# Layer 2 of an encoder trunk on 8 cores: another order of folding, statistics, gate tiles and shift transfers

## The reference, cut to what matters

```python
for i in range(DEPTH):
    shift, scale, gate = ada_modulation(c, w_ada[i], b_ada[i])   # silu(c) @ w + b, three parts
    h = rms_norm(x, g_norm[i]) * (1.0 + scale) + shift
    ...
    elif kind == 2:                      # layer 2, the one changed
        a, ag, z = jnp.split(jnp.einsum('bsd,de->bse', h, w_in_c), 3, axis=-1)
        glu = a * jax.nn.sigmoid(ag)
        ext, conv_c_new = with_history(glu, hist_c, CCONV_W - 1)       # 31 taps, depthwise
        y = causal_depthwise_conv(ext, w_conv_c) + b_conv_c
        y = jax.nn.silu(layer_norm(y, ln_c_g, ln_c_b))                 # over 2048 channels
        out = jnp.einsum('bse,ed->bsd', y * jax.nn.silu(z), w_out_c)
    x = x + gate * out
```

## Time and profile before

| what | value |
|---|---|
| median of 3 runs | 2197.24 us (2192.96 to 2240.93) |
| profiled execution | 2198.0 us, span 2196.5 us on core 0 |
| other cores' spans | 2178.1 to 2191.1 us |
| busy, core 0 | PE 94%, PE weight load 59%, DVE 48%, ACT 31%, POOL 14% |
| layer 2, g = 0 | about 1172 to 1498 us |
| layer 2, g = 1 | about 1498 to 1820 us |

### The profile page before, as it was taken

How to read it: one execution, slowest core, us unless ns; L and a number is a source line. 1 busy time by engine, 2 the same in 40 slices (tenths; PEclk the granted TensorE clock), 3 DMA queues, 4 the chain that set the end, 5 groups by cost and what they waited for, 6 DMA issues and landing times.

```text
span 2196.5 us, 38718 instructions; the slowest of 8 cores (2178.1 to 2196.5 us)
## 1 busy us (share of the span) xinstructions
PE 2073.5 (94%) x15725; PEld 1295.2 (59%) x15725; DVE 1044.8 (48%) x1463; ACT 685.4 (31%) x891; POOL 316.9 (14%) x605
## 2 busy tenths in 40 slices
PE   3999999999999999999999998999998999999996
PEld 1645666456666666666666664556564556666663
DVE  3454240542555554555545232555332657747745
ACT  3264313543011121111121434532445532222341
POOL 1001101011001000001003441103441100000000
PEclk9999999999999999999999999999999999999998
DMA  9836848078346543346446986667886743433347
GB/s 208 155 102 103 138 72 136 14 132 138 57 74 104 89 77 68 60 73 110 77 80 122 201 180 142 114 108 150 173 185 128 137 103 68 77 69 68 78 68 208
DMA packets 94064, 244.02 MB, mean 111 GB/s; under 512 B 17088, under 2 KB 42048, under 8 KB 93632
## 3 DMA queue, kind: packets, MB, share of 16 engines
q0 software_dynamic: 54992, 188.11, 48.6%
q1 hardware_dynamic: 38896, 53.43, 9.2%
HBM read 344.92 MB, written 13.76 MB: 163 GB/s over the span
## 4 chain that ended last, share of the span: by engine, by line
PE 83%; DMA 8%; DVE 3%; SPq 2%; ACT 2%; issue 2%; POOL 0%; DVEq 0%; ACTq 0%; POOLq 0%
PE ps L505 74%; PE ps L750 4%; DMA ring<-w_ada 2%; SPq L162 2%; PE ps L1120 2%; DMA ysT<-tmp 2%; DMA w_fold<-ring 1%; DMA ring<-w_in_a 1%; PE ps L1004 1%; PE ps L395 1%; DMA ring<-w_in_c 1%; PE ps L451 0%; DMA xa_sb<-xa 0%; PE ps L877 0%; DMA tmp<-tmp 0%
## 5 line engine op out<-in xcount | busy, mean ns | idle before, releaser
L505 PE MATMUL ps<-hT,ring 128*128 128x352 bf16 (+1 forms) x8448 | 1300.4, 315 | 22.0 <-DMA ring<-w_in_a 6.0
L505 PEld LDWEIGHTS ps<-hT,ring 128*128 128x128 bf16 x8448 | 826.0, 98 | 490.1 <-issue 40.3
L505 PE MATMUL ps<-ysT,ring 128*128 128x352 bf16 (+1 forms) x3072 | 470.4, 313 | 12.8 <-DVE xb_sb L594 5.1
L505 PEld LDWEIGHTS ps<-ysT,ring 128*128 128x128 bf16 x3072 | 297.8, 97 | 185.0 <-issue 21.4
L162 POOL DMA_DIRECT2D tmp<-tmp x256 | 129.5, 555 | 116.9 <-PE ps L1148 71.1
L750 PE MATMUL ps<-ring,hT 128*128 128x512 bf16 x544 | 123.6, 385 | 3.5 <-DMA ring<-w_in_a 2.7
L1073 DVE TENSOR_TENSOR tmp<-tmp,ps 128x1074 bf16<-128x1074 f32 (+3 forms) x64 | 45.5, 711 | 167.6 <-PE ps L505 160.9
L940 ACT ACTIVATE tmp<-ps 128x1074 f32<-128x1074 f32 (+1 forms) x32 | 33.9, 1059 | 263.7 <-PE ps L505 263.7
L951 DVE TENSOR_TENSOR tmp<-tmp,ps 128x1074 f32<-128x1074 f32 (+3 forms) x64 | 45.4, 709 | 140.4 <-PE ps L505 129.4
L1128 ACT ACTIVATE tmp<-ps,cst_sb 128x16 bf16<-128x16 f32 (+2 forms) x160 | 69.8, 437 | 111.4 <-PE ps L1120 87.8
L588 DVE SCALAR_TENSOR_TENSOR xb_sb<-ps,modT,xb_sb 128x1056 f32<-128x1056 f32 x32 | 42.2, 1317 | 119.6 <-PE ps L505 119.2
(11 more groups left out here) (182 smaller groups left out, 1619.9 us busy)
## 6 DMA issues: line engine op xcount, KB each, us to landing
ring<-w_in_b POOLq DMA_DIRECT2D x64, 512.0 KB, 5.3
ring<-w_ada POOLq DMA_DIRECT2D x48, 512.0 KB, 11.9
ring<-w_in_a POOLq DMA_DIRECT2D x48, 512.0 KB, 12.7
ring<-w_in_c POOLq DMA_DIRECT2D x48, 512.0 KB, 5.8
ring<-w_in_d POOLq DMA_DIRECT2D x24, 512.0 KB, 5.3
tmp<-tmp SPq DMA_DIRECT2D x128, 69.4 KB, 5.4
tmp<-tmp POOLq DMA_DIRECT2D x128, 69.4 KB, 5.7
tmp<-tmp SPq DMA_DIRECT2D x128, 67.5 KB, 5.0
```

The lines of the kernel that those rows point to most:

```text
L505: ins = h.matmul(PSB[:, 3 * sl + n, 0:W], lhsT=lw, rhs=rh[:, n * W:(n + 1) * W], start=(first and k == 0), stop=(last and k == len(pairs) ...
```

## The change

It has five parts. (1) In the loop, `square` and `stats` run five tiles behind instead of four; tile 11 is done in the tail. (2) Of the 16 shift transfers of a tile, 6 go over SP and 10 over POOL instead of 8 and 8. (3) The tail has another order; the first fold and the first batch of the second are emptied by DVE instead of ACT; the second fold's ring slots are taken after `zmm(4)`, its later batches come one gate tile later. (4) After `root`, the silu table is loaded by a one-column activation. (5) Part 1 of layer 3's modulation moves to hook 5 of layer 1, g = 1, and part 2 to hook 3 of layer 3, g = 0.

```diff
-        def batch(k):
-            if k == 0:
-                got["w"] = [get(sp) for sp in wspec]
-                got["o"] = [get(sp) for sp in ospec]
+        def take():
+            got["w"] = [get(sp) for sp in wspec]
+            got["o"] = [get(sp) for sp in ospec]
+
+        def batch(k, eng):
...
-                s.op("act", lambda h, o=o, hf=hf: h.activation(out=v3(o, 8)[:, 2 * k:2 * k + 2, :], in_=PSB[:, 3 * sl:3 * sl + 2, 256 * hf:256 * hf + 256], func=AF.Copy),
-                     writes=sk(sl) + [ok])
+                o, src = v3(o, 8)[:, 2 * k:2 * k + 2, :], PSB[:, 3 * sl:3 * sl + 2, 256 * hf:256 * hf + 256]
+                if eng == "act":
+                    s.op("act", lambda h, o=o, src=src: h.activation(out=o, in_=src, func=AF.Copy), writes=sk(sl) + [ok])
+                else:
+                    s.op("dve", lambda h, o=o, src=src: h.tensor_copy(out=o, in_=src), writes=sk(sl) + [ok])
...
-                parts.append((("sp", "pool")[r], "gr%d_%d" % (ci, r), moves, ["R%d.%d" % (ci, r)]))
+            for r, (q, lo, hi) in enumerate((("sp", 0, 6), ("pool", 6, 16))):
+                parts.append((q, "gr%d_%d" % (ci, r), moves[lo:hi], ["R%d.%d" % (ci, r)]))
...
-            if i >= 4:
-                square(i - 4)
+            if i >= 5:
+                square(i - 5)
             if i >= 2:
                 conv(i - 2)
-            if i >= 4:
-                stats(i - 4)
+            if i >= 5:
+                stats(i - 5)
...
+        square(11)
         conv(14)
         gather(14)
+        stats(11)
         square(12)
         zmm(0)
-        fa(0)
+        fa_take()
+        fa(0, "dve")
         stats(12)
-        square(13)
-        fa(1)
-        fa(2)
+        fa(1, "dve")
         conv(15)
         gather(15)
+        square(13)
         stats(13)
+        zmm(1)
         square(14)
-        zmm(1)
-        fa(3)
+        fa(2, "dve")
         stats(14)
+        fa(3, "dve")
         zmm(2)
         square(15)
         stats(15)
...
         root()
+        warm_table(AF.Silu)
         for c in range(3):
             center(c)
-        fb(0)
         zmm(4)
+        fb_take()
+        fb(0, "dve")
...
-                if c + 4 in (6, 8, 10):
-                    fb(c // 2)
+                if c + 4 in (7, 9, 11):
+                    fb((c - 1) // 2, "act")
...
-             (1, 1): {3: [(3, 0)]},
-             (2, 0): {14: [(3, 1)]},
-             (2, 1): {14: [(3, 2)]}}
-    SCR = {0: L0_AT, 1: 6528, 2: 8896}
+             (1, 1): {3: [(3, 0)], 5: [(3, 1)]},
+             (3, 0): {3: [(3, 2)]}}
+    SCR = {0: L0_AT, 1: 6528, 3: 8000}
```

More of the change, by code:

```diff
@@ L1025, in batch @@
                     release(sp)
-        return batch
+        return take, batch
     def in_phase2(g, hook):
@@ L1091, in spread @@
             parts = []
+            moves = []
             for r in range(2):
-                moves = []
                 for j in range(8):
@@ L1224, in in_phase2 @@
                 gather(i - 2)
-        fa, fb = [fold(q) for q in ((3, 2), (1, 0))[g]]
+        (fa_take, fa), (fb_take, fb) = [fold(q) for q in ((3, 2), (1, 0))[g]]
+        square(11)
         conv(14)
         gather(14)
+        stats(11)
         square(12)
         zmm(0)
-        fa(0)
+        fa_take()
+        fa(0, "dve")
         stats(12)
-        square(13)
-        fa(1)
-        fa(2)
+        fa(1, "dve")
         conv(15)
         gather(15)
+        square(13)
         stats(13)
+        zmm(1)
         square(14)
-        zmm(1)
-        fa(3)
+        fa(2, "dve")
         stats(14)
+        fa(3, "dve")
         zmm(2)
```

## The result

The changed kernel takes 2174.9 us (median), the kernel before 2196.5 us in the same comparison: a ratio of 0.988, with a 95% interval of 0.984 to 0.992. That is 21.6 us faster; 29.8 were forecast, and 2174.9 lies in the range of 2152 to 2187, within the two per cent of no change to which I had given 0.88. The profiled execution has a span of 2171.6 us, and its slowest core is core 2. The slowest core changes from execution to execution: the time to layer 1's first output projection alone differs by 8 to 14 us between the cores of one execution, in every kernel.

The account below looks back on a forecast made before the run. PE, busy 94% of the span, was taken as the bound, so time could be won only at its waits and low clock. 2198.0 - 17.6 - 8.7 - 8.3 + 4.8 = 2168.2 us, range 2152 to 2187.

Parts of the forecast that it names:

- A: End of each group in layer 2: moving the modulation removes weight waits, later waits and slow stretches; -17.6 us.
- B: Gate tiles 4 and 5 of layer 2: new ring-slot order and early silu table load remove waits; -8.7 us.
- C: Layer 2's loop: statistics a tile later no longer wait for gathers, and a slow stretch goes; -8.3 us.
- D: Start of layer 2's tail: added statistics waits outweigh the last convolution's lost slot waits; +4.8 us, between +3 and +9.
- R1: Layer 2's tail: half is given back, clock low at gate tiles 4 to 6, D costs 9; 2180 us, chance 0.20.
- R2: Layer 2's tail and convolutions: earlier gathers also remove slow stretches and shift waits; 2153 us, chance 0.13.
- R3: Layer 2's convolutions: POOL's part of the shifts lands late, each waits 2.4 us; 2240 us, chance 0.04.
- R4: Layers 1 and 3: the moved modulation does not hide and waits there, 11 us in all; 2179 us, chance 0.05.

Follow-up runs that it names:

- e1: The kernel before with part 5 alone (modulation parts moved to layers 1 and 3): 2177.3 us, ratio 0.991.
- e9: e1 with two lines more, the silu table loaded after `root` and `zmm(4)` before `fb(0)`: 2170.0 us, ratio 0.986.
- e7: The changed kernel without the early silu table load after `root`: 2177.6 us, ratio 0.992.
- e8: The changed kernel with `fb_take()` and `fb(0, "dve")` before `zmm(4)` again: 2179.5 us, ratio 0.991.
- e4: The changed kernel with the statistics four tiles behind again, no `square(11)` and `stats(11)` in the tail: 2179.3 us, ratio 0.990.
- e5: The changed kernel with the head of the tail reordered, PE's other work put where it waited for ACT: 2155.8 us, ratio 0.981.
- e3: The changed kernel with the 16 shift transfers split 8 and 8 over SP and POOL again: 2178.2 us, ratio 0.992.
- e10: e5 with the statistics four tiles behind again: 2153.4 us, ratio 0.980.
- e11: e5 with the shift transfers split 8 and 8 over SP and POOL: 2156.8 us, ratio 0.980.

## Why the prediction was right, and where it was not

*Direction and range* were right, the size by three quarters: 21.6 us of 29.8. In the stretches, step by step from before over e1 and e9 to the changed kernel, A gave 2.1 us more than forecast, B 1.8 less, and C and D together 8.9 less. That the miss is not larger is in part luck: A's surplus, which I had not seen, covered a quarter of it.

*A* was forecast at -17.6 and measured at -19.7 (e1). Its steps stand in the trace: both weight waits are gone, layer 1 and layer 3 hide the 4 loads each (layer 1 gained 1.3 us in length, the matmuls and transposes themselves), the DVE chain follows at one gate tile's distance. The margin of 1 us before the last products was not there; a wait of 0.5 is left. So the stretch o0-c1 fell by 2.9 us where I had 3.75 (2.41 and 1.34), and the waits of g = 1 by 1.7 (from 1.04 and 1.16 to 0.5) where I had 2.4. What makes up for it: the slow gate tile 15 stands in both groups (4.9 and 5.0 us on the mean core before, 3.74 now), and I had counted it once.

*B* was -8.7 and measured -6.9 (e9), its cost to tile 5 right (0.85 in e9, 0.87 in the changed kernel, against 0.9). That either half could be undone in the final kernel almost free (e7, e8) I did not foresee.

*C* is the term that failed: -8.3 forecast. I read 5.8 us of waits and a slow stretch from core 0, the slowest core, which was the slowest partly because of them. On the other seven cores the statistics waited 0 to 2.2 us per group in the loop; on the mean core, with core 0 among them, it was 1.4 us in both groups together. I noted that C was least sure on other cores, and still summed core 0's. e4 shows that the loop did not need the fifth tile once the rest was changed: the statistics wait there on no core with four. What five tiles gave, 2.8 us against e4, lies in the tail.

*D* was +4.8. For the statistics its places and sizes were right: 1.32, 3.42 (3.5 forecast), 0.54 and the old 2.26 in g = 0, 4.13 (4.2 forecast) in g = 1; all in all 11.1 us more than in e9, 10.7 forecast. The last convolution lost its wait for the slot, as forecast, and waits for its shifts: 1.5 us on the mean core in g = 0 and 0.3 in g = 1, where I took 0.6 twice. Both groups together it waits 1.9 us against 7.8 in e9, so 5.9 less, the amount forecast (7.13 less 1.2). On the mean core before, though, it was 5.5: here too core 0 had more than the others. e4 shows what the wait for shifts is. PE comes earlier there and waits longer, but begins the convolution of g = 0 at 140.2 to 141.1 us after c0, against 139.9 to 141.8 in the changed kernel, when the tile has landed.

C and D together were forecast at -3.5 and measured at +5.4 (changed against e9). Of the 8.9 between them, 7.6 are C, of which only the 0.7 us of loop waits in e9 could be won; D's two sums account for 0.4, and the rest is not assigned.

*The signs.* One that I had named for a wrong prediction did show: convolutions wait for shift transfers more than once a group on cores 0 and 6 in g = 0 and on core 4 in g = 1. The other did not: the clock is up at gate tile 5 on every core.

*The rivals.* R1 named the right direction, half given back, but for its clock reason only in part: the clock is low at gate tile 3, not at 5 to 7. R2 did not come, since shift waits stayed; e5 shows that its 2153 was within reach by another order. R3 is refuted: POOL's transfers land in 3.9 us instead of 5.7. R4 did not happen.

*POOL's pauses.* The Trainium skill (SBUF — State Buffer, "SBUF: two separate sides") says that DVE and GpSimd share a port pair that one of them holds for a whole instruction; for DVE it names operations in a two-port mode and, against a GpSimd operation that reads SBUF, those with two inputs in SBUF. I had read the pauses of POOL's issues as agreeing with it, and the trace hardly does. The pauses that it charges to nothing else come to 3.9 us in layer 2 before and 6.1 after, but an instruction of DVE runs in only 0.7 and 0.2 to 0.5 us of them, and some 30 issues of POOL run wholly inside DVE's product of bf16 tiles. On core 2 of the changed kernel the product ends at 1286.63, with POOL issuing beside it, and the pause follows from 1287.46:

```profile
1285.40 1.23 DVE L1108 TENSOR_TENSOR tmp<-dmask,wrep_sb 128x1024 bf16<-128x1024 bf16 x1
1285.91 1.55 POOL L162 DMA_DIRECT2D tmp<-tmp  x3 [0.86 <-PE ps L1153]
1288.76 3.53 POOL L162 DMA_DIRECT2D tmp<-tmp  x7 [1.30 <-issue]
```

What the pauses are stays open; on PE's time e3 shows no cost of issuing more on POOL.

## What to carry to other kernels

A term read from the slowest core alone can be partly the accident that made it the slowest: read the same waits on all cores before they enter a sum. A change that moves work away from a place where PE waits for it can be worth more than one that reorders the rest; here two entries of a table gave nine tenths of the gain. When PE waits for a chain over another engine, ask what work of PE's own can stand before it. In this tail that was worth as much again as the whole change, and two finer settings, the lag and the split, no longer mattered beside it.

## What the runs showed that I had not expected

Several small waits can cost the clock too. In the changed kernel, waits of 3.4, 0.5 and 2.3 us lie in front of gate tile 3, and it takes 5.43 us instead of 3.75 on seven of eight cores in g = 0 and on four in g = 1. In e5 the same tail of g = 0 has no wait over 0.9 us on seven cores (one of 1.6 on the eighth), and gate tile 3 takes 3.75 us in both groups of all eight cores, as it does in e10 and e11. That filling the waits keeps the clock up is shown; which wait brings it down is not. Core 0 of the changed kernel has all of them in g = 0 and 2.0 us more before the last convolution, and keeps its 3.75. On the mean core, 8.1 of e5's 10.9 us in g = 0 are waits, and 2.8 are shorter matmuls. And the queue with more to do was not the later one: with 10 and 6 instead of 8 and 8, POOL's transfers land in 3.9 us instead of 5.7, although POOL issues more of them, and SP's in 5.1 instead of 5.4.
